# A two-block transformer on one core: modulation row summed on VectorE in the dense layer, two of its rows read back during the experts, one pass for two norms

## What is computed

```python
# first block, its end
x = x + moe_swiglu(rms_norm(x, moe_norm[j]), ...)
x = rms_norm(x, final_norm)                      # the norm "norm_final"
# second block, its start
ada = silu(c) @ w_ada + b_ada                    # c: (1, 1024), w_ada: (1024, 6144)
shift_a, scale_a, gate_a, shift_m, scale_m, gate_m = split(ada, 6)
h = rmsnorm(x, g_mix) * (1 + scale_a) + shift_a  # the norm "norm_2"
proj = h @ w_in
...
x = x + gate_a * (mix @ w_out)
h = rmsnorm(x, g_mlp) * (1 + scale_m) + shift_m
x = x + gate_m * (square(relu(h @ w_ff1)) @ w_ff2)
```

## Time and profile before

| | us |
|---|---|
| median of 3 runs (2118.25 to 2121.61) | 2119.11 |
| profiled execution | 2121.15 |
| its span | 2119.4 |
| TensorE busy | 1885.8 (89%) |
| VectorE busy | 1448.6 (68%) |
| ScalarE busy | 1130.5 (53%) |
| GpSimd busy | 394.1 (19%) |
| of it, multiplying rows by c (48) | 122.3 |
| of it, adding rows (48) | 155.2 |

### The profile page before, as it was taken

One profiled execution on the slowest core, in us unless ns is written; L12 is line 12 of the kernel. 1 busy time (PEld: TensorE's weight loads), 2 busy tenths in 40 slices (PEclk: granted clock), 3 DMA queues, 4 the chain that ended last, 5 costly groups with the idle time before them and its releaser, 6 DMA issues.

```text
span 2119.4 us, 23611 instructions
## 1 busy us (share of the span) xinstructions
PE 1885.8 (89%) x8924; PEld 1576.4 (74%) x8926; DVE 1448.6 (68%) x1048; ACT 1130.5 (53%) x1015; POOL 394.1 (19%) x242
## 2 busy tenths in 40 slices
PE   6967799986876899999999999999999498779995
PEld 4856588775866788888888888888888277659894
DVE  4455666673753788888888888888888353555553
ACT  5344344432142677777777777777777253333331
POOL 1004999997300000000000000000000100200000
PEclk9987899988576999999999999999999697679998
DMA  8524677766012799999999999999999643225540
GB/s 296 199 91 138 197 256 260 247 211 229 1 60 91 284 373 373 386 370 385 372 385 374 376 382 378 375 370 380 363 384 355 240 132 108 60 80 184 188 143 20
DMA packets 247030, 535.06 MB, mean 252 GB/s; under 512 B 17570, under 2 KB 57666, under 8 KB 246288
## 3 DMA queue, kind: packets, MB, share of 16 engines
q1 hardware_dynamic: 232048, 476.24, 62.4%
q0 software_dynamic: 14880, 57.49, 8.0%
HBM read 520.01 MB, written 13.65 MB: 252 GB/s over the span
## 4 chain that ended last, share of the span: by engine, by line
PE 62%; DVE 2%; ACT 1%; DMA 1%; issue 1%; POOL 0%; DVEq 0%; ACTq 0%; POOLq 0%
PE bank L1854 19%; PE bank L1855 19%; PE bank L1862 19%; PE bank L2125 1%; PE bank L1966 1%; PE bank L1879 1%; PE bank L1929 0%; PE bank L2227 0%; PE bank L2280 0%; DMA taken<-y_dram,y_row 0%; PE bank L2160 0%; ACT mix L849 0%; DMA ada<-ada_parts 0%; DVE mix L1252 0%; PE bank L1944 0%
## 5 line engine op out<-in xcount | busy, mean ns | idle before, releaser
L1231 DVE TENSOR_TENSOR w_lo<-raw,w_hi 128x2048 fp32r<-128x2048 f32 (+1 forms) x454 | 1092.6, 2409 | 269.0 <-ACT w_hi L839 264.1
L839 ACT ACTIVATE w_hi<-raw 128x2048 fp32r<-128x2048 f32 (+1 forms) x454 | 867.0, 1912 | 582.1 <-PE bank L1855 480.8
L1854 PE MATMUL bank<-w_hi,slot_hi 128*128 128x512 f32 x896 | 357.6, 399 | 5.1 <-ACT w_hi L839 2.6
L1855 PE MATMUL bank<-w_hi,slot_lo 128*128 128x512 f32 x896 | 351.8, 393 | 0.0
L1854 PE MATMUL bank<-w_hi,hT_hi 128*128 128x512 f32 (+2 forms) x864 | 306.0, 367 | 4.0 <-ACT w_hi L839 4.0
L1855 PE MATMUL bank<-w_hi,hT_lo 128*128 128x512 f32 (+2 forms) x864 | 302.2, 363 | 0.0
L1862 PE MATMUL bank<-w_lo,slot_hi 128*128 128x512 f32 x896 | 242.7, 393 | 0.7 <-DVE w_lo L1231 0.7
L1854 PEld LDWEIGHTS bank<-w_hi,slot_hi 128*128 128x128 f32 x896 | 169.1, 189 | 40.7 <-issue 5.9
L1862 PEld LDWEIGHTS bank<-w_lo,slot_hi 128*128 128x128 f32 x896 | 168.8, 188 | 38.1 <-DVE w_lo L1231 1.1
L1855 PEld LDWEIGHTS bank<-w_hi,slot_lo 128*128 128x128 f32 x896 | 169.2, 189 | 34.8
L1854 PEld LDWEIGHTS bank<-w_hi,hT_hi 128*128 128x128 f32 x864 | 170.0, 197 | 29.4 <-issue 2.9
(11 more groups left out here) (265 smaller groups left out, 1815.8 us busy)
## 6 DMA issues: line engine op xcount, KB each, us to landing
raw<-in_moe_w_gate_up SPq DMA_DIRECT2D x448, 512.0 KB, 5.6
raw<-in_moe_w_down SPq DMA_DIRECT2D x224, 512.0 KB, 5.4
raw<-in_w_ff SPq DMA_DIRECT2D x64, 512.0 KB, 4.2
work<-in_w_ada POOLq DMA_DIRECT2D x48, 512.0 KB, 4.2
raw<-in_dense_w_gate_up SPq DMA_DIRECT2D x44, 512.0 KB, 4.9
raw<-in_b_w_in SPq DMA_DIRECT2D x24, 512.0 KB, 4.8
raw<-in_w_in SPq DMA_DIRECT2D x24, 512.0 KB, 5.2
raw<-in_dense_w_down SPq DMA_DIRECT2D x22, 512.0 KB, 5.4
```

What stands on the lines that cost most here:

```text
L839: act.activation(w_hi[:, g % SPLIT, 0:n], raw[:, g % RING, 0:n], ACT.Copy).then_inc(R.hi, 1)
L1231: dve.tensor_tensor(w_lo[:, g % SPLIT, 0:n], raw[:, g % RING, 0:n], f32(w_hi[:, g % SPLIT, 0:n]), ALU.subtract).then_inc(R.lo, 1)
L1854: pe.matmul(out_, hi, w_hi[:, s, c:c + w], start=(start and n == 0), stop=False, skip_group_check=True)
L1855: mm = pe.matmul(out_, lo, w_hi[:, s, c:c + w], start=False, stop=False, skip_group_check=True)
```

## The change

- **The sum** moves from GpSimd to VectorE. `ada_sum(count)` takes the next rows; `mlp_round` calls it with 2 and 2, and in a round of six units with 2 and 3 more. One row is one pass: multiply by `c` for the first of eight (`tensor_scalar`), multiply and add for the others. The order of the 48 is changed to row by row (`a` outer, `k` inner). VectorE's dense loop is written out instead of being a hardware loop. GpSimd only issues the 48 loads into the same three buffers.
- **The sum over partitions** is done at the start of b_in: 12 matmuls with `one_row`, which is zero but for one column, so that half row `j` of the modulation lands in partition `j` of bank 0, as 12 x 512. VectorE adds the bias (12 x 512), and GpSimd stores 24 KB, `ada_dram`. The waits for `ada_stored` at the HGRN stage are gone. TensorE's b_in product waits for VectorE's bias addition, which uses bank 0.
- **Read back**: two rows (shift_a, scale_a) go to `ada_first`, on all partitions, during the experts; the other four behind them. The stage `ada` has no matmuls any more. The gathered rows `taken` are split into `taken_a` and `taken_b`, and tiles are added one after the other.
- **Two norms in one pass.** With r1 the reciprocal root of `norm_final`, u = x * gain, the second norm's mean square is r1^2 * mean(u^2). So ACT sums the squares of x and of u, and VectorE forms both factors at once; x = u * r1, and h = u * r1 * r2 * gain(1 + scale) + shift come from u directly.

The diff, cut:

```diff
-        def ada_sums(pool):
...
+        ADA_ROWS = N_ADA * KC
+        def ada_row(n):
+            return work[:, (N_ADA + n % ADA_BUFFERS) * D:(N_ADA + n % ADA_BUFFERS + 1) * D]
+        def ada_rows(pool):
+            weights = wide(A["w_ada_2"])
+            pool.wait_ge(*at("mix_a"))
+            pool.dma_start(ada_place(), A["b_ada_2"].rearrange("l (a n) -> (l a) n", n=512)).then_inc(ada_bias_in, 16)
+            for n in range(ADA_ROWS):
+                a, k = n // KC, n % KC
+                if n >= ADA_BUFFERS:
+                    pool.wait_ge(ada_ready, n - ADA_BUFFERS + 1)
+                pool.dma_start(ada_row(n), weights[:, k, a * D:(a + 1) * D]).then_inc(ada_in[n % ADA_BUFFERS], 16)
+            pool.wait_ge(*at("ada", "row"))
+            pool.dma_start(ada_dram, ada_place()).then_inc(ada_stored, 16)
...
                 for e in range(3):
                     gather(e)
+                load_ada(pool, ada_first[:, :, :], 0)
...
             if have("ada"):
                 pool.wait_ge(*at("experts done"))
-                pool.wait_ge(ada_stored, 16)
-                for n in range(N_ADA // 2):
-                    pool.dma_start(ada[:, 2 * n:2 * n + 2, :].rearrange("p a d -> p (a d)"),
-                                   ada_parts[:, 2 * n * D:(2 * n + 2) * D]).then_inc(ada_back[n], 16)
+                for n in range(1, N_ADA // 2):
+                    load_ada(pool, ada[:, 2 * n - 2:2 * n, :], n)
...
             if have("hgrn"):
                 S.stage("hgrn")
-                if have("ada"):
-                    act.wait_ge(ada_stored, 16)
...
             if have("ada"):
                 S.stage("ada")
-                norm("norm_final", x, mix, at("experts done"))
-                ada_out(0, 6)
+                for t in range(TILES):
+                    act.wait_ge(*at("combined", 1, t))
+                    act.activation(plain[:, 1, t * D:(t + 1) * D], x[:, t, :], ACT.Square, accum_out=sums2[:, 0, t:t + 1])
+                    act.wait_ge(*at("gained", t))
+                    sq = act.activation(taken_a[:, t, :], mix[:, t, :], ACT.Square, accum_out=sums2[:, 1, t:t + 1])
+                sq.then_inc(S("norm_final", "squares"), 1)
+                act.wait_ge(*at("norm_final", "variance"))
+                act.activation(sums2[:, :, :], sums2[:, :, :], ACT.Sqrt).then_inc(S("norm_final", "deviation"), 1)
             if have("in_2"):
-                norm("norm_2", x, mix, at("norm_final", "h"))
-                ada_out(6, 12)
...
                 split_lo(R, g, rounds)
+                ada_sum(2)
                 split_lo(R, g + 1, rounds)
+                ada_sum(2)
                 split_lo(R, g + 2, rounds)
                 hidden(0)
                 if n == 2:
                     split_lo(R, g + 3, rounds)
                 hidden_lo(0)
                 if n == 2:
+                    ada_sum(2)
                     split_lo(R, g + 4, rounds)
                     hidden(1)
                     split_lo(R, g + 5, rounds)
                     hidden_lo(1)
+                    ada_sum(3)
...
                 turn_split("norm_b")
+                if have("ada"):
+                    dve.wait_ge(ada_bias_in, 16)
+                    dve.wait_ge(*at("ada", "summed"))
+                    dve.tensor_tensor(ada_place(), ada_place(), bank[0][0:2 * N_ADA, :], ALU.add).then_inc(S("ada", "row"), 1)
                 product("b_in", False)
             if have("hgrn"):
                 S.stage("hgrn")
-                if have("ada"):
-                    dve.wait_ge(ada_stored, 16)
...
+                for t in range(TILES):
+                    dve.wait_ge(y_taken[t], 32)
+                    for c in range(2):
+                        dve.scalar_tensor_tensor(out=x[:, t, :], in0=taken[c][:, t, :], scalar=ratio[:, 2 + c, t:t + 1],
+                                                 in1=x[:, t, :], op0=ALU.mult, op1=ALU.add).then_inc(S("combined", c, t), 1)
+                        dve.wait_ge(*S.last())
+                    dve.tensor_tensor(mix[:, t, :], x[:, t, :], g, ALU.mult).then_inc(S("gained", t), 1)
...
+                for t in range(TILES):
+                    dve.tensor_scalar(x[:, t, :], mix[:, t, :], mean[:, t:t + 1], None, ALU.mult)
+                    h = dve.scalar_tensor_tensor(out=plain[:, 0, t * D:(t + 1) * D], in0=mix[:, t, :], scalar=mean_u[:, t:t + 1],
+                                                 in1=ada_first[:, 1, :], op0=ALU.mult, op1=ALU.mult)
+                h.then_inc(S("gain used", 8), 1)
+                dve.wait_ge(*S.last())
+                for t in range(TILES):
+                    dve.tensor_tensor(mix[:, t, :], plain[:, 0, t * D:(t + 1) * D], ada_first[:, 0, :], ALU.add)\
+                       .then_inc(S("norm_2", "h", t), 1)
+                for n in (1, 2):
+                    dve.wait_ge(ada_back[n], 16)
...
             if have("b_in"):
                 S.stage("b_in")
+                if have("ada"):
+                    pe.wait_ge(ada_ready, ADA_ROWS)
+                    for j in range(2 * N_ADA):
+                        mm = pe.matmul(bank[0][0:2 * N_ADA, :], one_row[:, 2 * N_ADA - 1 - j:4 * N_ADA - 1 - j],
+                                       work[:, j * 512:(j + 1) * 512], start=(j == 0), stop=(j == 2 * N_ADA - 1))
+                    mm.then_inc(S("ada", "summed"), 1)
                 turn_split("norm_b", mix, at("norm_b", "h"))
+                if have("ada"):
+                    pe.wait_ge(*at("ada", "row"))
                 product("b_in", "norm_b")
...
-                turn_split("norm_2", mix, at("norm_2", "h"))
-                pe.wait_ge(*at("ada", "out", 11))
+                turn_split("norm_2", mix, at("norm_2", "h", TILES - 1))
```

More of the change, by code:

```diff
@@ L478, in program, with ada_place @@
         ff_loop = Loop("ff")
-        def ada_sums(pool):
-            acc = part(work, 0, N_ADA, D)
-            rows = part(work, N_ADA * D, ADA_BUFFERS, D)
+        def ada_place():
+            return work[0:2 * N_ADA, 9216:9728]
+        ADA_ROWS = N_ADA * KC
+        def ada_row(n):
+            return work[:, (N_ADA + n % ADA_BUFFERS) * D:(N_ADA + n % ADA_BUFFERS + 1) * D]
+        def ada_rows(pool):
             weights = wide(A["w_ada_2"])
             pool.wait_ge(*at("mix_a"))
[L487 to L517, removed]
@@ L967, in mlp_round @@
                     hidden_hi(1)
[L969 to L974, removed]
             def prepare():
@@ L1761, in _ @@
-                dve.wait_ge(*at("combined", 1, TILES - 1))
-                dve.memset(headsq[:, :], 1.0).then_inc(S("experts done"), 1)
+                dve.wait_ge(ada_back[0], 16)
+                g = gain_row(9)
+                scale = ada_first[:, 1, :]
+                dve.scalar_tensor_tensor(out=scale, in0=scale, scalar=1.0, in1=g, op0=ALU.add, op1=ALU.mult).then_inc(S("gain used", 9), 1)
+                g = gain_row(8)
+                dve.wait_ge(*at("route", "shares"))
+                for t in range(TILES):
[5 more added lines that the diff above has]
+                    dve.tensor_tensor(mix[:, t, :], x[:, t, :], g, ALU.mult).then_inc(S("gained", t), 1)
@@ L1763, in _ @@
+                S.also("experts done")
             if have("ada"):
                 S.stage("ada")
-                norm("norm_final", x, x, 8)
-                dve.wait_ge(*at("ada", "out", 3))
+                mean, mean_u = sums2[:, 0, :], sums2[:, 1, :]
+                dve.wait_ge(*at("norm_final", "squares"))
+                dve.tensor_scalar(sums2[:, :, :], sums2[:, :, :], 1.0 / D, None, ALU.mult).then_inc(S(), 1)
+                dve.wait_ge(*S.last())
+                dve.tensor_scalar(mean, mean, EPS, None, ALU.add).then_inc(S(), 1)
@@ L1767, in _ @@
+                dve.wait_ge(*S.last())
+                dve.scalar_tensor_tensor(out=mean_u, in0=mean, scalar=EPS, in1=mean_u, op0=ALU.mult, op1=ALU.add)\
+                   .then_inc(S("norm_final", "variance"), 1)
+                dve.wait_ge(*at("norm_final", "deviation"))
+                dve.reciprocal(sums2[:, :, :], sums2[:, :, :]).then_inc(S(), 1)
+                dve.wait_ge(*S.last())
             if have("in_2"):
                 S.stage("in_2")
-                norm("norm_2", x, mix, 9, 0)
@@ L1770, in _ @@
-                dve.wait_ge(*at("ada", "out", 11))
+                for t in range(TILES):
[3 more added lines that the diff above has]
+                h.then_inc(S("gain used", 8), 1)
+                dve.wait_ge(*S.last())
@@ L2219, in _ @@
                     experts(more_ring, more_loop, 1)
-            if have("ada"):
-                S.stage("ada")
-                pe.wait_ge(*at("experts done"))
-                for j in range(2 * N_ADA):
-                    pe.wait_ge(ada_back[j // 4], 16)
-                    if j >= 6:
-                        pe.wait_ge(*at("ada", "out", j - 6))
-                    pe.matmul(bank[j % 6][:, :], ones[:, :], ada[:, j // 2, j % 2 * 512:(j % 2 + 1) * 512], start=True, stop=True)\
```

(4 more changed lines are left out.)

70 lines of the change are left out of this document (44 added, 26 removed).

## The result

The changed kernel takes **2106.3 us** (median of 5 runs, 2102.0 to 2110.0) against 2119.6 for the kernel before beside it: ratio 0.994, 95% interval 0.993 to 0.996. It is faster, by 13 us and not by 30; 2106.3 lies outside the range of the prediction. The profiled execution took 2110.03, span 2108.2.

A forecast was written before the change was run, and what follows sets the result against it. TensorE was taken as the bound in the dense layer and experts, so only gaps between stages could gain: -2.4 + 1.7 - 17.8 - 11.3 = -29.8 us, giving a median of 2089.3 us, range 2081 to 2101.

The forecast's parts named there:

- Experts. [...] 0: Expert stretch: one more gain row, its 1 MB load and a 1.28 us VectorE pass are hidden; cost 0.
- Norm ahead of dense, -2.4: Entry to the dense layer: the norm's two VectorE passes fall from 4.91 to 2.56 us, saving 2.4 us.
- Dense layer, 0: Dense layer: 48 row sums added to VectorE fit beside TensorE's rounds of 33.69 us; cost 0.
- Waits of up to 1 us [...] inside its reserve: Dense layer: VectorE waits up to 1 us for a burst's row loads, without holding up TensorE.
- rival 1: Dense layer: VectorE falls behind at times, passing TensorE 1 to 2 us per round; 2094 to 2099 us, chance 0.12.
- 2.5 us for every row: Dense layer: by the skill's port-lock rule, each row load issued from GpSimd would come 2.5 us later; forecast took 0.
- Entry to b_in, +1.7: Ahead of b_in's first product: 12 matmuls eat the norm's saving and the bias pass adds a wait; 1.7 us longer.
- rival 3: Start of b_in: the 12-row matmuls run at half clock, +10 us, 2099 us; chance 0.08.
- HGRN, -17.8: HGRN stage: both waits for the modulation store go, so ACT's first copy follows the first turn; saves 17.8 us.
- rival 5: HGRN stage: another wait takes a third of the gain, 2095 us; chance 0.07.
- Behind the experts, -11.3: Behind the experts: merged norms and removed ones-matmuls start the normed rows' turn at 1691.7 instead of 1702.99, saving 11.3 us.
- rival 4: Behind the experts: the later modulation rows land late, at 15 us instead of 8; +5 us, 2094 us, chance 0.12.

The follow-up runs named there:

- The kernel with the two edits of order: Changed kernel with 192 unused bytes, plus fourth modulation row summed behind the first round's hidden products and bias pass ahead of the four low parts: 2079.5 us.

## Why the prediction was wrong

**The step that failed is "Experts. [...] 0"**, and with it the zero for everything behind. I costed the instructions that the change adds to a stage and not what its declarations do to the places of those that stay. 4680 products have a stationary operand in the moved buffers (3 x 896 with `slot`, 3 x 448 with `e_hid`, 3 x 216 with `hid`, by the groups of the profile); at 233.4 - 229.2 = 4.2 ns each that is 19.7 us. 16.9 of it are the experts' (`slot`, `e_hid`); `hid` is the dense layer's and the second feed-forward's, where the sum had nothing for it either. The changed kernel with and without 128 more bytes differs by 2106.3 - 2086.5 = 19.8, and the kernel before loses 2137.6 - 2118.6 = 19.0 by the same shift. No rival of mine held this.

**The sum, at equal distance, was right.** The changed kernel with its large buffers at the old distance takes 2086.5 us, 32 less than before; the sum said 29.8, and 2086.5 is inside the range. That it came out so close is in part luck: in the table the dense layer lost 1.7 us that the sum did not have, and the stretch behind the experts gained 1.4 more than it had. Term by term:

- *Norm ahead of dense, -2.4:* the table gives -2.4.
- *Dense layer, 0:* +1.7 at the old distance. "Waits of up to 1 us [...] inside its reserve" failed in the first round. Its fourth row's buffer came free at 229.5, and VectorE could use the row at 237.4, 8 us later; a row landed in 5.5 us in the median, where I had 4.2 from the easier stretch. There was no reserve there: TensorE had waited 0.93 us for the same hidden product before, since in a round of three units the hidden products follow at once. The other nine waits for rows in the same execution, up to 3.6 us long, reached TensorE nowhere: so rival 1 came once, in its mechanism, and not per round. The row issues took 0.53 to 0.56 us each, not more than before. 38 of the 48 ran beside a VectorE pass with two inputs, none beside a `tensor_scalar`. The Trainium skill ("SBUF — State Buffer", "SBUF: two separate sides") has descriptors wait for a VectorE operation in a two-port mode, and names passes with two SBUF inputs only against a GpSimd operation that reads SBUF. So the prediction's 2.5 us for every row read that rule too widely, and its argument from the issue times did not test the rule; no run here does. Why the landing was longer stays open.
- *Entry to b_in, +1.7:* +1.3. The 12 matmuls took 10.47 us at full clock (10.3 predicted, rival 3 out), the wait for the bias pass was 2.00, and the half-clock start behind it came as taken. The kernel with the two edits of order shows that this was a matter of order and not of need.
- *HGRN, -17.8:* 19.07 to 1.35, -17.7. Nothing else was late; rival 5 is out.
- *Behind the experts, -11.3:* -12.7 with 128 bytes more, -13.8 in the changed kernel. From the first combine to the turn both took 16.84 us, where the sum had 1691.7 - 1673.21 = 18.5. The two tensor_scalar passes took 0.75 us each where I took 1.28. There the trace agrees with the Trainium skill ("VectorE: DVE Perf Modes", "Mode 2×_2P — use both read ports for one tensor"), by which the term would have been -12.6; writing them with two inputs costs 0.95 us. The remaining 0.7 us are spread over the other passes and small steps. The 1.1 us between the two kernels are the gathered rows, which were there 12.5 us behind the last expert product in the changed kernel and 13.5 in the other; before it was 13.3, and no edit aimed at that. The four later rows were not late (rival 4 out).
- *Other stages:* between HGRN and the experts the changed kernel's profile is 2.6 us shorter, and the one with 128 bytes is not. Behind the turn of the normed rows the changed kernel is 4.6 us longer than before, of which the second feed-forward's 384 products explain 1.6 at 4.2 ns each. Differences of this size between single executions are the noise around this table.

## What to carry to other kernels

Before costing an edit, list what it declares: a 16-byte tensor ahead of large ones moves all of them. Here a pitch longer by 2% took back 19.8 of the 32 us that the removed waits were worth. In the trace, compare the distance of neighbouring LDWEIGHTS records between two kernels, by stationary operand, before looking for a new wait; busy time (944.86 and 947.04 of 950 us) and clock (1.00) hardly differed here. When one compares two orders of work, the stationary and moving operands should keep the same distance modulo 256 bytes in both, and at best distance 0.

## What the runs showed of the hardware that I had not expected

The pitch of fp32r matmuls of 128x512 depends on where the stationary operand begins relative to the moving one in the partition: 226.7 to 228.4 ns at distance 0 modulo 256, depending on the operand, 229.2 at 192, 231 to 234.5 at all other multiples of 32. It is a matter of the pair (moving 0 with stationary 128 is slow, 128 with 128 and 0 with 0 are fast) and the experts' mean repeats to 0.2 ns between kernels with equal distances. What in the chip makes it was not tried: whether the two reads meet in one part of the memory is a guess. Also open is why `slot_lo` products go at 228.4 and `e_hid` at 226.8 when both have distance 0.
